# An expert's Silu moved one matmul step forward, ahead of ScalarE's weight splits of that step

## The chip, the core and the metric

One core of a Trainium2 chip runs the whole program. The metric is the device time of one execution in microseconds (us), lower is better. A step or a wait named below is one of this core's engines: TensorE (PE, with its weight loads as PEld), VectorE (DVE), ScalarE (ACT), GpSimd (POOL) and SyncE (SP, which issues the large DMAs).

## What is computed

A two-layer trunk over 256 frames of width 1024. The first layer is a mixer and a dense SwiGLU; the second is stick-breaking attention and a mixture of eight experts, of which each frame uses two. The change touches the experts alone:

```python
def swiglu(x, w1, w3, w2):
    return (jax.nn.silu(x @ w1) * (x @ w3)) @ w2

    # moe_swiglu, D_FF = 2816
    for e in range(N_EXPERTS):
        y = y + combine[:, e:e + 1] * swiglu(xf, w1[e], w3[e], w2[e])
```

## The kernel before

The experts are sorted by their number of frames into eight places q. At an even q ("big") the expert has room for 128 frames and works in two halves of its 2816 hidden columns; at an odd q ("small") it has room for 64 frames and works in one go. Each half, or each small expert, is a phase n: twelve phases, of which 2, 5, 8 and 11 are small. Each phase has an up part and a down part, and the list `WORK` interlaces them: up 0, up 1, down 0, up 2, down 1, up 3, down 2, and so on. So after up n comes down n-1, except at the start, where up 1 follows up 0 directly.

An up part has 16 steps j. Step j takes one block of 128 rows (j // 2) of one matrix (j % 2: 0 is the gate matrix w1, 1 is w3). The gate matrix gathers in PSUM banks 0 to 2, w3 in banks 3 to 5. Step 14 completes the gate matrix, step 15 completes w3. A down part has 11 steps for a big expert and 22 for a small one.

For big experts every weight block is split into a rounded part and a remainder, so that a float32 product is made of three faster ones (L571 to L573). ACT writes the rounded part (`split_step_hi`, L831), then DVE the remainder (`split_step_lo`, L1842). The room for split blocks is small. The planner `place_units` therefore says for each block after which step its room is free, and the table `BEHIND[s]` lists the blocks that ACT and DVE split after step s. Small experts use their weights unsplit (L1664, L1685).

ACT and DVE walk through the same list of steps as PE, each with its own program order. After up n they do three things. ACT applies Silu to the gate banks and writes `u_act` (`silu_up(n)`, L1076, three instructions at L1080 of 512, 512 and 384 columns). DVE multiplies `u_act` by the w3 banks (`gate_up(n)`, L2266, L2270). PE turns the result by transposes (`turn_up(n)`, L1621) ahead of step 3 of the down part of a big expert, or step 4 of a small one. In phase 0 there is no down part in between: PE's step 0 of up 1 waits for `silu_up(0)`, because it overwrites the gate banks, and its step 1 waits for `gate_up(0)`, because it overwrites the w3 banks.

Both calls stand at the first step after up n, and so behind the blocks of `BEHIND` of step 15. By the planner's table five phases have blocks listed behind steps 14 and 15 of their up part:

| phase n | behind step 14 | behind step 15 |
|---|---|---|
| 0 | up 1 step 2 | up 1 step 3 |
| 1 | down 0 step 2 | down 0 steps 3, 4 |
| 4 | down 3 step 3 | down 3 step 4 |
| 7 | down 6 steps 2, 3 | down 6 step 4 |
| 10 | down 9 steps 2, 3 | down 9 steps 4, 5 |

In the other seven phases nothing is listed behind step 15. SP issues the weight loads in order. Each waits until the ring space that it overwrites is free: `lo_done` counts remainders written by DVE, `raw_used` counts steps of small experts done by PE (L643).

Of the kernel before, what the change touches and what calls it, by code (L numbers as in the profile page):

```python
# [22 lines left out]
def trunk(nc, x, e_norm1, e_w_in, e_sgu_ln_g, e_sgu_ln_b, e_sgu_w, e_sgu_b, e_conv_w, e_a_log,  # L23
# [4 lines left out]
    TILES, DC = SEQ // P, D // P  # L28
# [75 lines left out]
    def big(q):  # L104
        return q % 2 == 0
# [9 lines left out]
    STEPS, PIECES, n_big, n_raw = [], [], 0, 0  # L115
# [96 lines left out]
    def place_units():  # L212

        taken = [((i % SPLITS) * DC * CW, (i % SPLITS + 1) * DC * CW, i) for i in range(A_MOE - SPLITS, A_MOE)]
        at, spot, behind = (A_MOE % SPLITS) * DC * CW, {}, {}
        raws_needed = [raws for _, _, raws in WHERE]
        raw_step = [s for s, st in enumerate(STEPS) if not st.big]
        step_of = {A_MOE + st.at: s for s, st in enumerate(STEPS) if st.big}
        for s, st in enumerate(STEPS):
            if not st.big:  # L220
                continue
            if at + st.size > SPLIT_ROOM:
                at = 0
            last = max(claim(taken, at, at + st.size, A_MOE + st.at))
            spot[st.at] = (at, last)
            raws = max(raws_needed[:st.pieces[0][0] + 1])
            free = step_of.get(last, last - A_MOE)
            if raws:
                free = max(free, raw_step[raws - 1])
            if s > st.j and not STEPS[s - st.j - 1].big:  # L230
                start = s - st.j
                free = max(free, start if st.kind == "down" and st.j >= 4 else start - EARLY if st.kind == "up" else 0)
            behind.setdefault(free, []).append(s)
            at += st.size
        return spot, behind
# [14 lines left out]
    with ExitStack() as ctx:  # L250
# [269 lines left out]
        def stepped(eng, st):  # L520

            if st.big:
                eng.wait_ge(piece_used, A_MOE + st.at + 1)
            else:
                eng.wait_ge(raw_used, st.at + 1)

        def last_step(kind, n):
            return next(st for st in STEPS if st.kind == kind and st.n == n and st.ends)
# [8 lines left out]
        def gather_bank(q, b):  # L537
            return 6 + b if q == 0 else 3 + b
# [13 lines left out]
        def finished_before(st):  # L552

            v = STEPS.index(st)
            if st.j == 0 and v and STEPS[v - 1].kind == "down":
                p = STEPS[v - 1]
                if LAST[p.q] == p.n:
                    return p.q
            return None
# [219 lines left out]
        def _(act):  # L779
# [46 lines left out]
            def split_step_hi(st):  # L826

                (v, off), = st.pieces
                act.wait_ge(ring_in[arrive_sem(v)], arrive_count(v))
                used(act, SPOT[st.at][1])  # L830
                act.activation(unit(all_hi, st), in_ring(WHERE[v][0] + off, st.size), ACT.Copy).then_inc(hi_done, 1)  # L831
# [230 lines left out]
            def gathered(q):  # L1062

                for b in range(2):
                    act.wait_ge(gather_done, 2 * q + b + 1)
                    src = ps[:, gather_bank(q, b), :]
                    if big(q):
                        ins = act.activation(xg_hi[:, 4 * b:4 * b + 4, :], src.rearrange("p (c n) -> p c n", c=4), ACT.Copy)
                    else:
                        ins = act.activation(xg_raw[:, 4 * b:4 * b + 4, :], src[:, 0:4 * SMALL].rearrange("p (c n) -> p c n", c=4),  # L1070
                                             ACT.Copy)
                    ins.then_inc(xgh_ready, 1)

            def silu_up(n):

                stepped(act, last_step("up", n))  # L1076
                if n:
                    act.wait_ge(hT_done, TURN0 + PARTS * n)
                for b, (c0, w) in enumerate(UP_COLS):
                    act.activation(u_act[:, c0:c0 + w], ps[:, b, 0:w], ACT.Silu).then_inc(silu_done, 1)  # L1080

            def turned_hi(n, parts=range(PARTS)):

                for b in parts:
                    act.wait_ge(hT_done, TURN0 + PARTS * n + b + 1)
                    blocks = turn_blocks(b)
                    src = ps[:, turn_bank(n, b), 0:P * len(blocks)].rearrange("p (j n) -> p j n", n=P)
                    m = m_hi if big(PHASE[n][0]) else m_raw
                    act.activation(m[n % 2][:, blocks[0]:blocks[-1] + 1, :], src, ACT.Copy).then_inc(hTh_ready, 1)

            def finished(q):

                stepped(act, last_step("down", LAST[q]))
                if big(q):
                    ins = act.activation(y_exp[:, 512:D], ps[:, 7, :], ACT.Copy)
                else:
                    ins = act.activation(y_small[SMALL:P, :], ps[SMALL:P, 6, :], ACT.Copy)
                ins.then_inc(y_act, 1)

            gathered(0)  # L1100
            for s, st in enumerate(STEPS):
                if finished_before(st) is not None:
                    finished(finished_before(st))
                if st.kind == "up" and st.n == 1:
                    if st.j == 0:
                        silu_up(0)
                    if st.j == 3:
                        turned_hi(0, (0, 1))
                    if st.j == 7:
                        turned_hi(0, (2,))  # L1110
                if st.kind == "down" and st.n + 1 < PHASES:
                    q = PHASE[st.n + 1][0]
                    if st.j == 0:
                        silu_up(st.n + 1)
                    if st.j == TURN_AT[st.big]:
                        turned_hi(st.n + 1)
                    if st.j == GATHER_AT and LAST[q] == st.n + 1 and q + 1 < NE:
                        gathered(q + 1)
                for k in BEHIND.get(s, ()):
                    split_step_hi(STEPS[k])  # L1120
            finished(NE - 1)
# [673 lines left out]
        def _(vec):  # L1795
# [469 lines left out]

            def gate_up(n):  # L2266

                for b, (c0, w) in enumerate(UP_COLS):
                    vec.wait_ge(silu_done, ACT0 + PARTS * n + b + 1)
                    tt(u_act[:, c0:c0 + w], u_act[:, c0:c0 + w], ps[:, 3 + b, 0:w], ALU.mult).then_inc(act_ready, 1)  # L2270
# [19 lines left out]
            def finished(q):  # L2290

                stepped(vec, last_step("down", LAST[q]))
                if big(q):
                    ins = vec.tensor_copy(y_exp[:, 0:512], ps[:, 6, :])
                else:
                    ins = vec.tensor_copy(y_small[0:SMALL, :], ps[0:SMALL, 6, :])
                ins.then_inc(y_vec, 1)
# [12 lines left out]
            for s, st in enumerate(STEPS):  # L2310
# [13 lines left out]
                if st.kind == "up" and st.n == 1:  # L2324
                    if st.j == 0:
                        gate_up(0)
                    if st.j == 3:
                        turned_lo(0, (0, 1))
                    if st.j == 7:
                        turned_lo(0, (2,))  # L2330
# [111 lines left out]
```

## Time and profile before

| | |
|---|---|
| median of 3 runs | 1226.92 us (1224.8 to 1231.65) |
| the profiled execution, its own time | 1229.17 us |
| its span, first to last instruction | 1227.1 us |
| PE busy | 1162.8 us, 95% of the span |
| DVE busy | 665.1 us, 54% |
| ACT busy | 559.7 us, 46% |
| mean granted TensorE clock | 0.986 |
| HBM read | 348.89 MB |

The experts take roughly the second half of the span, from 511 us on. In that half the page shows 360 to 416 GB/s in most of its slices of 30.7 us, so that PE and the DMA engines look full at the same time. A mean over a slice can't tell which of the two is waiting for the other. For that the rows below are read: they name single waits, single instructions and short stretches.

### The profile page before, as it was taken

What the parts mean: (1) busy time and instruction counts of PE and PEld (TensorE: products, weight loads), DVE (VectorE), ACT (ScalarE), POOL (GpSimd) and SP (SyncE); (2) the same over time, 40 slices, a digit from 0 to 9 for tenths busy, and PEclk for the clock granted to TensorE, in tenths of its full rate; (3) what the DMA queues carried; (4) which work ended last, traced back from release to release, by engine and by line L of the source; (5) the groups of instructions that cost most, each with busy time, mean ns of one, the idle gap of its engine ahead of it and who ended that gap; (6) DMA issues with size and microseconds to landing.
All of it is one profiled execution on the core that took longest, in us unless ns stands there. A gap on an engine that the chain in (4) does not pass through costs nothing.

```text
span 1227.1 us, 16270 instructions
## 1 busy us (share of the span) xinstructions
PE 1162.8 (95%) x6555; PEld 858.4 (70%) x6555; DVE 665.1 (54%) x736; ACT 559.7 (46%) x638; POOL 49.6 (4%) x93
## 2 busy tenths in 40 slices
PE   5989899999999999899998999999999989999986
PEld 5979778888879886778637748548568368386351
DVE  4866655545455422797507658038476058474053
ACT  4772454344444565476407547036355056263041
POOL 8010000000000121000000000000000000000000
PEclk9999999999999999899999999999999989999998
DMA  9632259655554421298799999999999999998993
GB/s 318 185 105 71 69 183 364 209 191 182 177 170 151 166 71 64 89 360 292 263 416 413 411 414 413 397 412 414 411 398 377 374 412 412 401 412 323 416 409 128
DMA packets 116736, 351.07 MB, mean 286 GB/s; under 512 B 8136, under 2 KB 55280, under 8 KB 116656
## 3 DMA queue, kind: packets, MB, share of 16 engines
q1 hardware_dynamic: 115552, 347.11, 74.3%
q0 software_dynamic: 1104, 2.86, 0.8%
q8 instruction: 54, 0.88, 0.3%
q14 instruction: 26, 0.21, 0.0%
HBM read 348.89 MB, written 1.05 MB: 285 GB/s over the span
## 4 chain that ended last, share of the span: by engine, by line
PE 84%; DMA 6%; DVE 4%; ACT 3%; POOL 2%; issue 1%; POOLq 0%; SPq 0%; DVEq 0%; ACTq 0%
PE ps L571 20%; PE ps L573 19%; PE ps L572 19%; PE ps L1664 8%; PE ps L1685 6%; DMA arena_c<-in_o_moe_w_dram 5%; PE ps L1609 3%; PE ps L1646 2%; DVE all_lo L1842 1%; PE ps L1621 1%; PE ps L1318 1%; POOL level L689 1%; PE ps L1526 1%; ACT all_hi L831 1%; PE ps L1538 1%
## 5 line engine op out<-in xcount | busy, mean ns | idle before, releaser
L1842 DVE TENSOR_TENSOR all_lo<-arena_c,all_hi 128x1408 fp32r<-128x1408 f32 (+1 forms) x120 | 170.7, 1448 | 217.4 <-ACT all_hi L831 217.3
L831 ACT ACTIVATE all_hi<-arena_c 128x1408 fp32r<-128x1408 f32 (+1 forms) x120 | 146.5, 1246 | 246.3 <-DMA arena_c<-in_o_moe_w_dram 199.9
L1842 DVE TENSOR_TENSOR all_lo<-arena_a,all_hi 128x1408 fp32r<-128x1408 f32 (+1 forms) x96 | 138.2, 1471 | 24.7 <-ACT all_hi L831 24.4
L571 PE MATMUL ps<-all_hi,xg_hi 128*128 128x512 f32 (+1 forms) x384 | 144.9, 377 | 2.9 <-ACT u_act L1080 2.9
L573 PE MATMUL ps<-all_hi,xg_lo 128*128 128x512 f32 (+1 forms) x384 | 144.8, 377 | 0.0
L831 ACT ACTIVATE all_hi<-arena_a 128x1408 fp32r<-128x1408 f32 (+1 forms) x96 | 119.2, 1262 | 56.0 <-PE ps L573 35.3
L572 PE MATMUL ps<-all_lo,xg_hi 128*128 128x512 f32 (+1 forms) x384 | 144.4, 376 | 0.0
L571 PE MATMUL ps<-all_hi,x_hi 128*128 128x512 f32 (+1 forms) x336 | 124.2, 370 | 5.1 <-ACT xn L920 2.4
L1835 DVE TENSOR_TENSOR all_lo<-arena_a,all_hi 128x2048 fp32r<-128x2048 f32 x40 | 91.4, 2289 | 58.0 <-ACT all_hi L824 58.0
L573 PE MATMUL ps<-all_hi,x_lo 128*128 128x512 f32 (+1 forms) x336 | 120.8, 360 | 0.0
L572 PE MATMUL ps<-all_lo,x_hi 128*128 128x512 f32 (+1 forms) x336 | 120.7, 359 | 0.0
L1664 PE MATMUL ps<-arena_c,xg_raw 128*64 128x512 f32 (+1 forms) x408 | 91.9, 558 | 0.3 <-DMA arena_c<-in_o_moe_w_dram 0.2
L571 PE MATMUL ps<-x_hi,all_hi 128*128 128x256 f32 x288 | 84.4, 293 | 4.3 <-DVE x_lo L1828 3.3
L824 ACT ACTIVATE all_hi<-arena_a 128x2048 fp32r<-128x2048 f32 x40 | 76.5, 1914 | 25.6 <-PE ps L573 21.7
L1664 PE MATMUL ps<-arena_a,xg_raw 128*64 128x512 f32 x360 | 82.9, 558 | 2.3 <-DMA arena_a<-in_o_moe_w_dram 2.3
L571 PEld LDWEIGHTS ps<-all_hi,xg_hi 128*128 128x128 f32 x384 | 72.5, 189 | 16.8 <-ACT u_act L1080 3.2
L571 PE MATMUL ps<-all_hi,m_hi 128*128 128x512 f32 x176 | 73.7, 419 | 9.9 <-DVE all_lo L1842 9.9
L572 PE MATMUL ps<-x_lo,all_hi 128*128 128x256 f32 x288 | 82.6, 287 | 0.0
L573 PE MATMUL ps<-x_hi,all_lo 128*128 128x256 f32 x288 | 82.6, 287 | 0.0
L572 PEld LDWEIGHTS ps<-all_lo,xg_hi 128*128 128x128 f32 x384 | 72.5, 189 | 11.9
L573 PEld LDWEIGHTS ps<-all_hi,xg_lo 128*128 128x128 f32 x384 | 72.5, 189 | 11.3
L1835 DVE TENSOR_TENSOR all_lo<-arena_c,all_hi 128x2048 fp32r<-128x2048 f32 x25 | 57.3, 2291 | 35.8 <-ACT all_hi L824 35.8
(367 smaller groups left out, 1782.2 us busy)
## 6 DMA issues: line engine op xcount, KB each, us to landing
arena_c<-in_o_moe_w_dram SPq DMA_DIRECT2D x136, 704.0 KB, 9.9
arena_a<-in_o_moe_w_dram SPq DMA_DIRECT2D x120, 704.0 KB, 9.8
arena_c<-in_o_moe_w_dram SPq DMA_DIRECT2D x45, 1024.0 KB, 15.3
arena_a<-in_o_moe_w_dram SPq DMA_DIRECT2D x35, 1024.0 KB, 16.1
arena_c<-in_e_ffn_w_dram SPq DMA_DIRECT2D x36, 512.0 KB, 6.9
arena_a<-in_e_ffn_w_dram SPq DMA_DIRECT2D x30, 512.0 KB, 5.1
arena_a<-in_e_w_in_dram SPq DMA_DIRECT2D x24, 512.0 KB, 8.8
arena_a<-in_o_w_qkv_dram SPq DMA_DIRECT2D x12, 512.0 KB, 4.5
```

The source lines that it names most:

```text
L571: pe.matmul(o, a_hi, b_hi, start=first, stop=False)
L572: pe.matmul(o, a_hi, b_lo, start=False, stop=False)
L573: return pe.matmul(o, a_lo, b_hi, start=False, stop=last)
L689: after(pool.affine_select(out=t, in_=t, pattern=pattern, compare_op=op, fill=fill, base=base, channel_multiplier=cm))
L824: act.activation(w_hi[i % SPLITS][:, :], ring[slot][:, :], ACT.Copy).then_inc(hi_done, 1)
L831: act.activation(unit(all_hi, st), in_ring(WHERE[v][0] + off, st.size), ACT.Copy).then_inc(hi_done, 1)
L1609: last = mm(ps[:, gather_bank(q, c // 4), at:at + n], xn[:, t, c * P:(c + 1) * P], sel_p[:, t, 0:n], start=(t == 0), stop=(t == TILES - 1))
L1646: mm(ps[:, SCAT[q][m], :], a, y, start=True, stop=True).then_inc(scat_done, 1)
L1664: last = mm(ps[a * SMALL:(a + 1) * SMALL, o + b, 0:n], xg_raw[:, c, :], raw[a][:, c0:c0 + n], start=(c == 0), stop=(c == DC - 1))
L1685: last = mm(ps[hf * SMALL:(hf + 1) * SMALL, 6, :], m_raw[st.n % 2][:, j, st.a * SMALL:(st.a + 1) * SMALL], raw[:, hf * 512:(hf + 1) * 512] ...
L1835: tt(w_lo[i % SPLITS][:, :], ring[slot][:, :], w_hi[i % SPLITS][:, :].bitcast(F32), ALU.subtract).then_inc(lo_done, 1)
L1842: tt(unit(all_lo, st), in_ring(WHERE[v][0] + off, st.size), unit(all_hi, st).bitcast(F32), ALU.subtract).then_inc(lo_done, 1)
```

## The change

`silu_up(n)` waits for step 14 of up n (found by the new `gates_step(n)`) instead of step 15. In ACT's program it moves from the first step after up n to step 15 of up n itself, ahead of the blocks that `BEHIND` lists there. `gate_up(n)` stays where it is in DVE's program. Since Silu no longer implies that w3's banks are complete, it gets a wait of its own for step 15.

```diff
+        def gates_step(n):
+            return next(st for st in STEPS if st.kind == "up" and st.n == n and st.part == (DC - 1, 0))
+
         def last_step(kind, n):
...
             def silu_up(n):
 
-                stepped(act, last_step("up", n))
+                stepped(act, gates_step(n))
                 if n:
                     act.wait_ge(hT_done, TURN0 + PARTS * n)
...
                 if st.kind == "up" and st.n == 1:
-                    if st.j == 0:
-                        silu_up(0)
                     if st.j == 3:
                         turned_hi(0, (0, 1))
...
                 if st.kind == "down" and st.n + 1 < PHASES:
                     q = PHASE[st.n + 1][0]
-                    if st.j == 0:
-                        silu_up(st.n + 1)
                     if st.j == TURN_AT[st.big]:
                         turned_hi(st.n + 1)
...
+                if st.kind == "up" and st.j == 2 * DC - 1:
+                    silu_up(st.n)
                 for k in BEHIND.get(s, ()):
                     split_step_hi(STEPS[k])
...
             def gate_up(n):
 
+                stepped(vec, last_step("up", n))
                 for b, (c0, w) in enumerate(UP_COLS):
```

## Rows read from the trace of the kernel before

**Rows 1.** PE's waits, 540 to 1215 us: waiting, awaited, total, times, longest.

```profile
PE ps L571 <- DVE all_lo L1842: 9.9, 4, 3.0
PE ps L1621 <- DVE u_act L2270: 3.6, 4, 1.4
```

**Rows 2.** Windows: PE, PEld, DVE, ACT, POOL busy; clock, DMA share, GB/s.

```profile
604.00:606.00 2.00, 2.00 (x10) 1.53 (x9) 0.00 (x0) 0.00 (x0) 0.00 (x0) 1.00 0.01 3
...
780.00:782.00 2.00, 2.00 (x12) 0.72 (x10) 0.00 (x0) 0.00 (x0) 0.00 (x0) 1.00 0.72 237
...
1126.00:1128.00 2.00, 2.00 (x10) 1.05 (x10) 0.00 (x0) 0.00 (x0) 0.00 (x0) 1.00 0.00 0
```

**Rows 3.** ACT's timeline: start, us, line, out<-in, count, idle before and releaser.

```profile
546.55 1.39 ACT L831 ACTIVATE all_hi<-arena_c 128x1408 fp32r<-128x1408 f32 x1 [0.53 <-PE ps L573]
548.46 1.38 ACT L831 ACTIVATE all_hi<-arena_c 128x1408 fp32r<-128x1408 f32 x1 [0.53 <-PE ps L573]
...
583.06 1.06 ACT L831 ACTIVATE all_hi<-arena_c 128x1024 fp32r<-128x1024 f32 x1 [0.85 <-PE ps L573]
...
586.89 1.45 ACT L1080 ACTIVATE u_act<-ps 128x512 f32<-128x512 f32 x3
588.21 1.07 ACT L831 ACTIVATE all_hi<-arena_c 128x1024 fp32r<-128x1024 f32 x1
...
752.89 2.98 ACT L831 ACTIVATE all_hi<-arena_a 128x1024 fp32r<-128x1024 f32 x3 [0.85 <-PE ps L573]
...
927.64 2.98 ACT L831 ACTIVATE all_hi<-arena_c 128x1024 fp32r<-128x1024 f32 x3 [0.85 <-PE ps L573]
...
1103.66 2.01 ACT L831 ACTIVATE all_hi<-arena_a 128x1024 fp32r<-128x1024 f32 x2 [0.85 <-PE ps L573]
```

**Rows 4.** DVE's timeline around the ends of up 0, 1, 4, 7, 10.

```profile
549.87 1.63 DVE L1842 TENSOR_TENSOR all_lo<-arena_c,all_hi 128x1408 fp32r<-128x1408 f32 x1 [0.29 <-ACT all_hi L831]
551.42 1.74 DVE L2270 TENSOR_TENSOR u_act<-u_act,ps 128x512 f32<-128x512 f32 x3
...
586.07 2.36 DVE L1842 TENSOR_TENSOR all_lo<-arena_c,all_hi 128x1024 fp32r<-128x1024 f32 x2 [0.69 <-ACT all_hi L831]
...
757.82 1.23 DVE L1842 TENSOR_TENSOR all_lo<-arena_c,all_hi 128x1024 fp32r<-128x1024 f32 x1 [0.34 <-ACT all_hi L831]
...
928.74 3.50 DVE L1842 TENSOR_TENSOR all_lo<-arena_c,all_hi 128x1024 fp32r<-128x1024 f32 x3 [0.69 <-ACT all_hi L831]
...
1107.03 2.35 DVE L1842 TENSOR_TENSOR all_lo<-arena_c,all_hi 128x1024 fp32r<-128x1024 f32 x2
```

**Rows 5.** PE's timeline where PE first uses what Silu and the gate give.

```profile
551.25 0.80 PE L571 MATMUL ps<-all_hi,xg_hi 128*128 128x512 f32 x1 [2.88 <-ACT u_act L1080]
...
554.79 0.40 PE L571 MATMUL ps<-all_hi,xg_hi 128*128 128x512 f32 x1
...
590.15 1.42 PE L1621 MATMUL ps<-ident,u_act 128*128 128x128 f32 x11 [1.08 <-DVE u_act L2270]
...
760.76 0.98 PE L1621 MATMUL ps<-ident,u_act 128*128 128x128 f32 x7
...
933.95 1.31 PE L1621 MATMUL ps<-ident,u_act 128*128 128x128 f32 x10 [0.30 <-DVE u_act L2270]
...
1111.10 1.42 PE L1621 MATMUL ps<-ident,u_act 128*128 128x128 f32 x11 [1.43 <-DVE u_act L2270]
```

**Rows 6.** Windows behind five of PE's gaps; the clock is the third number from the end.

```profile
551.00:554.60 3.60, 3.35 (x8) 2.80 (x9) 2.16 (x4) 0.19 (x1) 0.00 (x0) 0.53 0.97 319
...
648.50:652.00 3.50, 3.50 (x15) 2.87 (x16) 3.30 (x4) 3.43 (x6) 0.00 (x0) 1.00 1.03 410
...
817.60:821.00 3.40, 3.37 (x8) 2.70 (x9) 3.19 (x3) 3.27 (x6) 0.00 (x0) 0.52 1.03 411
...
1111.00:1114.50 3.50, 3.40 (x21) 3.00 (x22) 3.50 (x5) 2.77 (x5) 0.00 (x0) 1.00 1.02 415
...
1169.00:1172.40 3.40, 3.40 (x10) 2.62 (x9) 3.33 (x4) 3.40 (x7) 0.00 (x0) 0.50 1.02 404
```

## The prediction

> **What bounds the kernel now.** I read three kinds of view in this order: the waits of PE, then short windows of the DMA engines, then the timelines of ACT and DVE where up parts end. PE is the engine that matters in the expert stage, and its list of waits is short [rows 1]: four waits for a weight remainder, 9.9 us together, and four transposes that waited for the gate product, 3.6 us together. The reader should see what is missing there. Silu itself is named nowhere in the list but once, at the end of up 0, where PE stood idle for 2.88 us [rows 5].
>
> The DMA engines look full over the stage, but they run dry behind every big expert. At 604 us they moved 3 GB/s, at 780 us they fell to a share of 0.72, and at 1126 us they moved nothing [rows 2]; a stretch like the first stands near 950 us. In those stretches SP waits for ring space that a small expert's steps free, so PE sets when the stream starts again. What PE loses between two such stretches therefore moves the next stream, the arrival of the next weights, and the end. I count each such loss in full.
>
> **What the change moves.** No instruction is added or removed. The three Silu instructions keep their cost: they start at 586.89 and the next instruction at 588.21, so they occupy ACT for 1.32 us, and the last ends after 1.45 us [rows 3]. No DMA is issued by what is moved, and no other queue is passed. What changes is the order on ACT: Silu now stands ahead of the splits behind step 15. DVE's order stays: remainders of the blocks behind step 15 first, then the gate product. So the gate product no longer waits for a late Silu, but a remainder ahead of it waits for a rounded part that now stands behind Silu. In seven phases nothing is listed behind step 15. There ACT's order is as before and PE's transposes wait either for nothing or for remainders; I take 0 for them. DVE's added wait is for a step that Silu used to wait for; queued behind it are the gate product and later remainders, which have the same condition already. A further hop between engines is about 0.05 us, so the five waits are 0 to 0.25 us; I take 0, since each is met before the remainder ahead of it is done.
>
> **Phase 0.** Before, ACT splits at 546.55 and 548.46, one PE step of 1.91 us apart, and Silu follows the second [rows 3]. Now it follows the first, so PE starts up 1 at 551.25 - 1.91 = 549.34 and its gap shrinks from 2.88 to 0.97 us. That is the gain that one would expect. But step 1 of up 1 waits for the gate product. The second split now starts at 546.55 + 1.29 + 1.32 = 549.16 instead of 548.46, 0.70 us later (1.29 is a split's 1.38 less the 0.09 by which the next instruction overlaps it). Its remainder on DVE starts at 549.87 + 0.70 = 550.57 and the gate product at 551.42 + 0.70 = 552.12; it takes 1.74 us [rows 4], so PE may begin step 1 at 553.91. PE has finished step 0 at 549.34 + 1.91 = 551.25 and now waits 2.66 us there.
>
> Before, step 1 began at 554.79 [rows 5], because step 0 ran slowly: from 551 to 554.6 us, behind the gap of 2.88, a clock of 0.53 was granted, that is mostly the 1.2 GHz level [rows 6]. So step 0 took 554.79 - 551.25 = 3.54 us, 1.63 more than a full-speed step, and step 1 ended at 556.70. If the clock falls behind the new gap too, step 1 ends at 553.91 + 3.54 = 557.45, which is +0.75. If it does not, it ends at 555.82, which is -0.88. The new gap of 2.66 is nearest to the old one of 2.88, so I take +0.75 and keep -0.88 for the range.
>
> **Phases 1, 4, 7 and 10.** The same sum four times: when does the first split behind step 15 start, if Silu's 1.32 us are put ahead of it?
>
> Phase 1: the split behind step 14 starts at 583.06 and is followed by Silu 0.97 us later, at 584.03. The next split starts at 585.35, its remainder 1.10 us later (split and hand-over, 583.06's kind) at 586.45, against 586.07 [rows 3, 4]: +0.38. The transposes at 590.15 had waited 1.08 us for the gate product [rows 5], so PE is late by all of it.
>
> Phase 4: three splits from 752.89 end at 755.87; Silu begins at 755.78, the next split at 757.10, its remainder at 758.20 against 757.82: +0.38. PE reached these transposes at 760.76 without a wait; the gate product would end at about 761.08 and PE start 0.04 later, so +0.36.
>
> Phase 7: of the three splits from 927.64 two are behind step 14. They occupy ACT until 929.57, Silu until 930.89, and the third's remainder starts at 931.99. Before, it was the third of a run of three from 928.74 that took 3.50 us, so it began at 931.02 [rows 4]: +0.97. The transposes had waited 0.30 us already.
>
> Phase 10: two splits from 1103.66 occupy ACT until 1105.58, Silu until 1106.90, and the third remainder starts at 1108.00 against 1107.03: +0.97. The transposes' wait grows from 1.43 to 2.40 us.
>
> What hides none of this: in all four cases the gate product stands directly behind these remainders on DVE, and PE directly behind the gate product. If PE had slack there, it would show no idle time ahead of the transposes; only phase 4 shows none.
>
> The sum is 0.75 + 0.38 + 0.36 + 0.97 + 0.97 = 3.43 us.
>
> **The clock behind the fourth wait.** PE's gap of 2.40 us in phase 10 is one the trace of before does not have at that place. Behind 1.43 us there the clock stayed at 1.00. Of the four waits for a remainder the longest took 3.0 of 9.9 us [rows 1], so the other three took 2.3 each. The windows from 648.5, 817.6 and 1169 us lie behind those three: 1.00 was granted in the first, 0.52 and 0.50 in the others [rows 6]. So two of three fell. The price is between 0 and 1.63 us; by those rows, the nearest in length, I take two thirds, 1.1 us. Total 3.43 + 1.1 = 4.5 us.
>
> Against the profiled execution that is 1229.17 + 4.5 = 1233.7. That execution lies 2.25 us above the median of the runs, inside their scatter, so for the median I add the same sum: 1226.92 + 4.5 = **1231.4 us**.
>
> **The rivals.** First, the stream of weights absorbs it. For this speak the full DMA windows outside the dry stretches; against it the three windows where the engines stood or sagged. It would give no change, 1226.9 us. The Trainium skill, page "Perfetto Trace Analysis", section "Roofline", says that a single core can pull about 120% of its 358 GB/s share and is then held by its 16 DMA engines. By that rule a stage this full is set by its bytes, and PE's microsecond would cost nothing. The trace agrees on the rate, with 410 to 415 GB/s in three of the windows read for the clock [rows 6], but not on the conclusion, since the rate falls to 3 and 0 in others.
>
> Second, the first boundary keeps the full clock, or the splits behind it are less delayed than I think: phase 0 gives -0.88 instead of +0.75, and the sum falls to 1.8, or 2.9 with the clock's part: 1228.7 to 1229.8 us.
>
> Third, the expected gain arrives. PE starts up 1 earlier by 1.91 us at full clock, saving 1.63 more, and the later delays are absorbed: -3.5, or 1223.4 us. For it speaks the one wait for Silu, against it the order on DVE, which puts a remainder ahead of the gate product.
>
> Fourth, on the slow side: the clock. It decides in phases 1, 7 and 10, where PE's gaps grow to 1.46, 1.27 and 2.40 us. If it falls behind all three, that is 3 x 1.63 = 4.9 on top of 3.43, so +8.3 and 1235.3 us. From two falls on, the sum passes 6.1 us. Against it: behind 1.43 us at 1111 it did not fall.
>
> **How the numbers follow.** 0.5% is 6.1 us, about what a measurement of this kernel can tell from no change. Forecast 0.55, first rival 0.10, second 0.14, third 0.08, fourth 0.13. The runs of before scatter from 1224.8 to 1231.65, so the forecast's upper part, some 0.13, and most of the fourth lie over 1233.1: slower 0.24. Faster by over 6.1 us only the third could give, and only with scatter: 0.05. The rest, 0.71, is within. The range from 1226.0 to 1236.0 takes in the forecast with both ends of the clock's price, the first two rivals and the fourth.
>
> **What would show it.** In the trace after: Silu's three instructions at about 547.8 and PE's start of up 1 near 549.3; a second gap of about 2.7 us ahead of step 1 of up 1, named as a wait for the gate product; waits of transposes for the gate product of 1.5, 0.4, 1.3 and 2.4 us in phases 1, 4, 7 and 10; dry stretches of the DMA engines that each begin and end later by the sum so far. The prediction is wrong if the remainders behind step 15 start no later than before, if the second gap in phase 0 is missing, or if the dry stretches end where they did while PE's waits have grown.

## The result, and the profile after

| | before | after |
|---|---|---|
| median | 1229.38 us (1223.76 to 1232.55, 9 runs) | 1237.11 us (1234.13 to 1238.85, 9 runs) |
| ratio | | 1.0071, 95% interval 1.005 to 1.0091 |
| profiled execution, span | 1227.1 us | 1236.5 us |
| instructions in it | 16270 | 16282 |

The change makes the kernel slower by 8.7 us (6.1 to 11.2). The forecast was 4.5 us: the right sign, half the size, and the time lies above the stated range. The ratios here and below compare the executions as a whole; the microseconds beside them follow the ratio and differ from the difference of the two medians by up to 1.2 us. The three Silu instructions do what the diff says. What they cost, and what else the change brought along, is read in the profile after. Its span is 9.4 us longer.

PE's timeline after, at the places of [rows 5], with the first matmul of the expert stage ahead of them and the last scatter behind:

```profile
514.28 0.98 PE L1610 MATMUL ps<-sel_p,xn 128*128 128x128 f32 x3 [0.42 <-DVE sel_p L2179]
...
552.34 0.50 PE L574 MATMUL ps<-all_hi,xg_hi 128*128 128x512 f32 x1 [0.97 <-ACT u_act L1083]
...
556.93 0.54 PE L574 MATMUL ps<-all_hi,xg_hi 128*128 128x512 f32 x1 [2.42 <-DVE u_act L2272]
...
594.35 1.42 PE L1622 MATMUL ps<-ident,u_act 128*128 128x128 f32 x11 [1.46 <-DVE u_act L2272]
...
766.16 1.42 PE L1622 MATMUL ps<-ident,u_act 128*128 128x128 f32 x11 [0.46 <-DVE u_act L2272]
...
940.56 1.42 PE L1622 MATMUL ps<-ident,u_act 128*128 128x128 f32 x11 [1.41 <-DVE u_act L2272]
...
1117.22 2.61 PE L1622 MATMUL ps<-ident,u_act 128*128 128x128 f32 x11 [2.55 <-DVE u_act L2272]
...
1222.86 1.99 PE L1647 MATMUL ps<-y_small,back_last 64*128 64x512 f32 x8 [0.89 <-DVE y_small L2298]
```

The gap before up 1 has shrunk from 2.88 to 0.97 us, and a second one of 2.42 us has opened behind it, which waits for the gate product. Ahead of the transposes the gaps have grown from 1.08, 0, 0.30 and 1.43 to 1.46, 0.46, 1.41 and 2.55 us.

ACT after, at the end of up 0:

```profile
547.63 1.39 ACT L834 ACTIVATE all_hi<-arena_c 128x1408 fp32r<-128x1408 f32 x1 [0.53 <-PE ps L576]
549.55 1.39 ACT L834 ACTIVATE all_hi<-arena_c 128x1408 fp32r<-128x1408 f32 x1 [0.53 <-PE ps L576]
550.85 1.44 ACT L1083 ACTIVATE u_act<-ps 128x512 f32<-128x512 f32 x3
552.16 1.40 ACT L834 ACTIVATE all_hi<-arena_c 128x1408 fp32r<-128x1408 f32 x1
```

DVE after, the same stretch:

```profile
553.59 1.63 DVE L1843 TENSOR_TENSOR all_lo<-arena_c,all_hi 128x1408 fp32r<-128x1408 f32 x1 [0.99 <-ACT all_hi L834]
555.13 1.74 DVE L2272 TENSOR_TENSOR u_act<-u_act,ps 128x512 f32<-128x512 f32 x3
```

The reader should see the order: split, Silu, split on ACT; and on DVE an idle time of 0.99 us that waits for the second of these splits, with the gate product behind it. The w3 banks had been complete since PE's last matmul of up 0 (552.34 - 0.97 = 551.37), Silu was done at 552.29, and the product began at 555.13.

At the end of the program ACT waits for VectorE's queue, in the profile before and then after:

```profile
1219.37 1.06 ACT L794 ACTIVATE xn<-h 128x1024 f32<-128x1024 f32 x1 [2.05 <-DVEq L2411]
```

```profile
1228.81 1.06 ACT L797 ACTIVATE xn<-h 128x1024 f32<-128x1024 f32 x1 [4.31 <-DVEq L2413]
```

That is 2.26 us more. VectorE jumps here over the loop for further items, which is not entered. From the end of the jump's record to VectorE's next one pass 0.53 us before and 2.82 us after. Its last addition runs on for 0.6 us from there in both profiles: before, that covers the jump, and after, VectorE computes nothing for the other 2.2 us.

The third place lies ahead of the experts, where the change does nothing. The first matmul of the expert stage stands at 514.28 after and in the next row before:

```profile
511.09 1.20 PE L1609 MATMUL ps<-sel_p,xn 128*128 128x128 f32 x4 [0.42 <-DVE sel_p L2178]
```

Windows after (columns as in [rows 2]; the clock is the third number from the end) show two stretches at the 1.2 GHz level there, behind gaps of 2.37 and 2.27 us that both kernels have, and two more behind gaps that the change made:

```profile
89.60:92.80 3.20, 3.20 (x18) 2.98 (x18) 0.00 (x0) 0.00 (x0) 0.00 (x0) 0.50 0.02 5
147.60:150.80 3.20, 3.09 (x7) 2.48 (x8) 3.20 (x2) 0.00 (x0) 0.00 (x0) 0.51 0.65 194
557.20:560.40 3.20, 3.20 (x10) 2.67 (x10) 1.21 (x1) 0.00 (x0) 0.00 (x0) 0.51 0.93 328
...
1117.00:1120.20 3.20, 2.98 (x13) 2.88 (x14) 3.20 (x4) 1.53 (x3) 0.00 (x0) 0.51 1.02 417
```

Before, the clock stayed up at the first two:

```profile
88.50:91.50 3.00, 3.00 (x35) 2.87 (x35) 0.00 (x0) 0.84 (x1) 0.00 (x0) 1.00 0.02 5
146.50:149.50 3.00, 3.00 (x13) 2.26 (x13) 3.00 (x2) 0.00 (x0) 0.00 (x0) 1.00 0.80 260
```

So the span's 9.4 us divide into 3.19 ahead of the experts (514.28 - 511.09), 3.99 within them (1222.86 - 1215.68 - 3.19, the last scatter of before being at 1215.68), and 2.26 at the jump. Whether the first and the last belong to the change is for the runs to say.

### The profile page after: what moved, and what is told of

It reads as the page before. It is cut to its first block, busy times and chain, and to the rows that moved or that the text cites. A ratio compares the mean times of both kernels' runs of the same rounds, so it can differ in the third digit from the quotient of the medians.

```text
span 1236.5 us, 16282 instructions
## 1 busy us (share of the span) xinstructions
PE 1164.7 (94%) x6555; PEld 860.0 (70%) x6555; DVE 665.4 (54%) x736; ACT 560.2 (45%) x638; POOL 49.7 (4%) x93
## 4 chain that ended last, share of the span: by engine, by line
PE 83%; DMA 6%; DVE 4%; ACT 3%; issue 2%; POOL 2%; POOLq 0%; SPq 0%; ACTq 0%; DVEq 0%
PE ps L574 19%; PE ps L576 19%; PE ps L575 19%; PE ps L1665 8%; PE ps L1686 6%; DMA arena_c<-in_o_moe_w_dram 4%; PE ps L1610 3%; PE ps L1647 2%; PE ps L1622 1%; DMA arena_a<-in_o_moe_w_dram 1%; PE ps L1319 1%; ACT all_hi L834 1%; DVE u_act L2272 1%; POOL level L692 1%; PE ps L1527 1%
## 5 line engine op out<-in xcount | busy, mean ns | idle before, releaser
L574 PEld LDWEIGHTS ps<-all_hi,xg_hi 128*128 128x128 f32 x384 | 72.6, 189 | 17.1 <-DVE u_act L2272 2.7
L574 PEld LDWEIGHTS ps<-all_hi,x_hi 128*128 128x128 f32 x336 | 64.3, 191 | 17.9 <-issue 5.6
```

The lines of the kernel that those rows point to most:

```text
L574: pe.matmul(o, a_hi, b_hi, start=first, stop=False)
```

## The experiments

Theory A says that two things belong to the change. On ACT, a split that DVE's gate product indirectly waits for now stands behind Silu. And the twelve waits added on VectorE lengthen the jump at the end. Theory B puts the loss on the added waits in the experts; theory C calls the end chance; a fourth puts 3 us ahead of the experts. All runs carry out the whole computation.

**Only the waits.** The kernel before, and in it

```diff
             def gate_up(n):
 
+                stepped(vec, last_step("up", n))
                 for b, (c0, w) in enumerate(UP_COLS):
```

> The kernel before, with nothing of the change but the wait for step 15 ahead of each of the twelve gate products on VectorE; Silu stands where it stood. Theory A (the changed kernel loses in two places: about 4 us in the experts through the order on ScalarE, and 2.3 us at the end, where VectorE's jump over the unused loop takes 2.9 us instead of 0.6 because twelve more instructions moved its target): the experts keep the gaps of before (2.88 us before up 1, 1.08, 0.30 and 1.43 us before the transposes of phases 1, 7, 10), the jump takes about 2.9 us, and the time is 2.3 us above before. Theory B (the added waits cost in the experts): the transposes' gaps grow and the jump stays at 0.6 us. Theory C (the 2.3 us at the end are chance): nothing moves, time as before.

Measured: 1231.45 us against 1229.52, ratio 1.0019 (1.0008 to 1.003), which is +2.3 us. PE's gaps before up 1 and before the transposes of phases 1, 7 and 10 are 2.88, 1.08, 0.30 and 1.43 us, those of before. All waits of transposes for the gate product make 4.8 us against 3.6 [rows 1]; the rest lies in small phases, where gaps of about 0.8 us come and go in every kernel (6.2 us in all in "the target of the jump" below, which executes the instructions of before). The end is that of the changed kernel:

```profile
1222.75 1.06 ACT L794 ACTIVATE xn<-h 128x1024 f32<-128x1024 f32 x1 [4.30 <-DVEq L2412]
```

The waits cost nothing that can be seen where they stand, and 2.3 us at the jump. B and C fall.

**Only the order.** The changed kernel without the waits on VectorE:

```diff
-                stepped(act, gates_step(n))
+                stepped(act, gates_step(n) if SPLIT_AFTER(n) else last_step("up", n))
...
             def gate_up(n):
 
-                stepped(vec, last_step("up", n))
```

`SPLIT_AFTER(n)` is true for phases 0, 1, 4, 7 and 10. There a remainder ahead of the gate product on VectorE already implies step 15.

> The change's order on ScalarE without the added VectorE instructions. Silu stands ahead of the splits of step 15; in the five phases with splits there it waits for step 14, in the other seven for step 15 as before, so that the gate products need no wait of their own. Theory A: PE's gaps are those of the changed kernel (0.97 us before up 1 and 2.4 us before its step 1; 1.46, 0.46, 1.41 and 2.55 us before the transposes of phases 1, 4, 7, 10), the jump at the end takes 0.6 us, and the time lies 3 to 6 us above before and 2.3 us below the changed kernel. Theory B (the added waits carry the loss): gaps and time as before. A theory in which 3 us of the loss lie ahead of the experts whatever the instructions: 6 to 8 us above before.

Measured: 1234.37 us, ratio 1.0046 (1.0032 to 1.006), +5.6 us. PE's gaps are those of the changed kernel: 0.96 and 2.44 in phase 0, then 1.47, 0.47, 1.41 and 2.55. ACT's wait for the jump is 2.05 us as before. In this profile the first matmul of the experts stands at 511.20, with no stretch of low clock behind those two gaps: the 3.19 us of the other profile are not of the change. Over the twelve profiles of this document this place follows the number of such low stretches between 22 and 505 us and not the edit: 511.1 to 511.2 with none, 512.4 to 513.1 with one, 514.3 to 515.2 with two, 515.6 with three. Order and waits together make 1.0065; the change measured 1.0071.

**The complement: the gate product first.** In the changed kernel VectorE's order is changed in the same way:

```diff
-                    if st.j == 0:
-                        gate_up(0)
...
-                        if st.j == 0:
-                            gate_up(following)
...
+                if st.kind == "up" and st.j == 2 * DC - 1:
+                    gate_up(st.n)
                 for k in BEHIND.get(s, ()):
                     split_step_lo(STEPS[k])
```

> The changed kernel, with VectorE's order changed in the same way: the gate product of up n stands ahead of the remainders behind step 15, with its wait for step 15. Theory A (what costs is the remainder that stands ahead of the gate product and now waits for a rounded part behind Silu): the wait of 2.4 us before step 1 of up 1 falls under 0.5 us, the transposes' gaps in phases 1, 4, 7 and 10 go to about 0, the jump at the end keeps its 2.9 us; up 1 gains about 3.5 us and the transposes 2.8 us on the kernel before, the end gives 2.3 us back: about 4 us below before. Rival (PE then waits for the late remainders themselves): gaps of 1 us or more appear ahead of down steps 3 or 4 or of up 1 step 3, and the time is no lower than before.

Measured: 1225.05 us, ratio 0.9966 (0.9953 to 0.9979), -4.2 us. This is PE's list of waits, 540 to 1215 us:

```profile
PE ps L574 <- DVE all_lo L1843: 10.3, 4, 3.3
PE ps L1665 <- DMA arena_a<-in_o_moe_w_dram: 1.7, 2, 0.9
PE ps L1686 <- DVE y_exp L2296: 1.0, 1, 1.0
PE ps L574 <- ACT u_act L1083: 1.0, 1, 1.0
...
PE ps L1622 <- DVE u_act L2272: 0.8, 1, 0.8
```

The wait before step 1 of up 1 is gone, and of the transposes' waits one of 0.8 us is left; it lies in phase 5, where nothing is listed behind step 15. The list of the changed kernel had 2.4 and 7.6 us in these two rows. No wait for a late remainder has come in their place: 10.3 us against 9.9 in [rows 1]. The remainder ahead of the gate product is the cause of the order's loss. The end is as slow as the twelve waits make it: here the jump took 3.05 us.

**The target of the jump.** The kernel before, with twelve waits in the loop that is jumped over:

```diff
                     k = vec.value_load(item_i[0:1, 1, bass.ds(it, 1)], min_val=0, max_val=NK - 1)
+                    for _ in range(12):
+                        vec.wait_ge(items_ready, 1)
                     prep_item(it, k)
```

> The kernel before with twelve waits added inside VectorE's loop for further items, which is not entered here: nothing more is executed, only the target of the jump over the loop lies twelve instructions further on. If the place of the target decides how long the jump takes: about 2.9 us instead of 0.6, time 2.3 us above before. If the place of the jump itself decides, or the number of instructions executed: 0.6 us, time as before.

Measured: 1230.57 us, ratio 1.0001 (0.9987 to 1.0015); ACT's wait 2.05 us, the jump 0.53. A target that alone lies twelve instructions further on costs nothing here.

**The gate product first, Silu at its old time.** As the complement, but with

```diff
-                stepped(act, gates_step(n))
+                stepped(act, last_step("up", n))
...
             def gate_up(n):
 
-                stepped(vec, last_step("up", n))
```

> Silu ahead of the splits behind step 15 and the gate product ahead of the remainders behind step 15, but Silu waits for step 15 as in the kernel before, so no wait is added on VectorE. Theory A (the remainder ahead of the gate product costs the experts' part, twelve added waits the end): the gap before up 1 is about 1.6 us instead of 0.97, none before its step 1, none before the transposes of phases 1, 4, 7 and 10; the jump at the end takes 0.6 us. Time about 6 us below before, and 1.5 us below the kernel with the gate product first and the waits. If the earlier start of Silu were what pays: a time like before.

Measured: 1224.76 us, ratio 0.9954 (0.9937 to 0.997), -5.7 us. The gap before up 1 is 1.56 us, and the transposes of phases 1, 4, 7 and 10 wait for nothing. So with Silu ahead of the splits the order on VectorE carries the gain, and Silu's earlier wait is worth 0.6 us at most, at up 1. VectorE's order changed alone, with Silu behind the splits, was not tried.

**The gate product first, waits in five phases only.** As the complement, with

```diff
-                stepped(act, gates_step(n))
+                stepped(act, gates_step(n) if SPLIT_AFTER(n) else last_step("up", n))
...
-                stepped(vec, last_step("up", n))
+                if SPLIT_AFTER(n):
+                    stepped(vec, last_step("up", n))
```

> Both orders changed as in the kernel with the gate product first; Silu waits for step 14, and VectorE has its wait for step 15, only in the five phases with splits behind step 15. Five instructions are added on VectorE instead of twelve. Gaps as in that kernel: 0.97 us before up 1 and none before the transposes. If the jump's cost comes in a step as its place moves on, it is 0.5 or 2.8 us and nothing between; if it grows with each instruction, about 1.5 us. Time 6.5 us below before in the first case, 4.3 in the second, 5.3 in the third.

Measured: 1222.89 us, ratio 0.9956 (0.994 to 0.9972), -5.4 us. This and the run ahead of it beat both kernels and can't be told apart. Five added instructions leave the jump at 0.53 us, so its cost does not grow with their number:

```profile
1213.13 1.06 ACT L800 ACTIVATE xn<-h 128x1024 f32<-128x1024 f32 x1 [2.05 <-DVEq L2415]
```

At the end of up 10, where the change had made the longest of the transposes' gaps, DVE now does two remainders, the gate product, then the rest:

```profile
1099.81 2.36 DVE L1846 TENSOR_TENSOR all_lo<-arena_a,all_hi 128x1024 fp32r<-128x1024 f32 x2 [0.69 <-ACT all_hi L837]
1102.08 1.74 DVE L2276 TENSOR_TENSOR u_act<-u_act,ps 128x512 f32<-128x512 f32 x3
1103.74 5.76 DVE L1846 TENSOR_TENSOR all_lo<-arena_c,all_hi 128x1024 fp32r<-128x1024 f32 x5
```

**Phase 0 alone.** The order of "only the order", in phase 0:

```diff
+                if st.kind == "up" and st.j == 2 * DC - 1 and st.n == 0:
+                    silu_up(st.n)
```

> The change's order and its earlier wait in phase 0 alone; Silu of the other eleven phases as before, no wait added. Forecast of the prediction for this part: +0.75 us with the clock falling behind the second gap, -0.88 without, so between 0.9 us below and 0.8 us above before; the gaps before up 1 and before its step 1 are 0.97 and 2.4 us, the transposes' gaps those of before (1.08, 0.30 and 1.43 us in phases 1, 7, 10). If phase 0 carries the loss: 3 us or more above before.

Measured: 1229.98 us, ratio 1.0011 (0.9999 to 1.0024), +1.4 us. The gaps are 0.97 and 2.42 in phase 0 and those of before elsewhere. The interval holds the forecast of +0.75 and leaves out -0.88. In this profile the clock did not fall behind the gap of 2.42 us; this execution, at 1227.79 us, was the second fastest of twelve.

**The later phases alone.** The same with `st.n > 0`.

> The change's order in phases 1 to 11, phase 0 as before, no wait added. Forecast of the prediction for this part: 0.38 + 0.36 + 0.97 + 0.97 = 2.7 us, and up to 1.6 us more for the clock in phase 10: 2.7 to 4.3 us above before. Gaps before the transposes 1.46, 0.46, 1.41 and 2.55 us in phases 1, 4, 7 and 10; 2.88 us before up 1. If phase 0 carries the loss: time as before.

Measured: 1233.59 us, ratio 1.0035 (1.0022 to 1.0048), +4.3 us. The gaps are 2.88 before up 1, and 1.47, 0.47, 1.41 and 2.55 before the transposes. The two halves, 1.0011 and 1.0035, make the 1.0046 of the whole order.

**How far the slow jump reaches.** The kernel before with more waits ahead of each gate product, in two sizes, each executed once:

```diff
             def gate_up(n):
 
+                for _ in range(3):                     # and 7 in the second
+                    stepped(vec, last_step("up", n))
```

> The kernel before with three waits instead of one ahead of each of the twelve gate products on VectorE: 36 instructions added, all of them met at once. So far the jump at the end took 0.5 us with 0 and 5 added instructions and 2.8 us with 12. If it is a step at one place in the program that recurs only much further on, 2.8 us here would say that the slow stretch is at least 24 instructions long, 0.5 us that it is shorter. If it grew with the number of instructions: 8 us.

> The same with seven waits ahead of each gate product: 84 instructions added. If the jump's cost depends on where it lies in some block of the program, either 0.5 or 2.8 us; if it grows with the number of instructions: over 15 us. PE's gaps in the experts stay those of the kernel before.

The 36 and 84 waits became 24 and 48 executed instructions: three waits take two instructions, seven take four. With 24 the jump took 2.78 us, the time was 1233.01 against 1225.47 of before beside it; the jump explains 2.2 of these 7.5 us, and single executions scatter by as much as the rest. With 48 it took 0.53 us and 1223.98. In order of added instructions, 0, 5, 12, 24 and 48, the jump took 0.53, 0.53, 2.82 (3.05 with the gate product first), 2.78 and 0.53 us. It is quick or slow with nothing between, and does not grow with the number: what the instructions change is the place of the jump and of its target together.

## Why the prediction was right and wrong

**Wrong: what the change adds.** The step that failed says that no instruction is added and that VectorE's waits are worth 0. The diff itself adds a wait, and twelve of them are twelve instructions on VectorE: 16282 against 16270. I priced them where they stand, and there the price of 0 held. I did not ask what else they move. They move everything behind them in VectorE's program, and the jump at the end went from 0.53 to 2.82 us. Run alone, they cost 2.3 us of the 8.7. The trace of before held the jump, ahead of the [2.05 <-DVEq] above, but not a slow one, so its price could not have been read there. That a place in VectorE's program has a price could have been asked: the Trainium skill, page "Runtime: NRT & Kernel Launch", section "Instruction fetch mechanics", says that a taken branch whose target lies outside the window already loaded must fetch it first. By that rule the wait is a fetch. The traces fit that. They list the DMA packets that carry instructions ("q14 instruction" on the page of the profile), and in all twelve profiles one of 8192 bytes starts 0.96 to 1.42 us behind the end of the jump's record. In the eight with a quick jump VectorE has gone on before it starts. In the four with a slow one VectorE goes on 1.82 to 1.84 us after its start, and where it started 0.23 us later than in the profile after, with the gate product first, the jump took 0.23 us longer. Which engine's instructions such a packet holds the trace does not say, and why 12 and 24 added instructions make the jump wait, and 5 and 48 do not, stays open; a target moved alone by twelve did not bring it.

**Wrong too: the base.** I added the sum to 1226.92 us, the median of three executions. The nine executions of before in the result have a median of 1229.38, 2.46 us more. The measured 1237.11 lies 1.1 us above the range's end of 1236.0, so either of the two, the jump or the base, was enough to carry it out. The base was a matter of scatter and says nothing of the mechanism; the jump is the part of it that was missed.

**Right: the order, its places and nearly its size.** The forecast without the jump was 4.5 us; order alone measured 5.6 (3.9 to 7.4). The parts:

| step of the prediction | forecast | in the profile after, or in a run alone |
|---|---|---|
| gap before up 1 | 0.97 us | 0.97 |
| gap before its step 1 | 2.66 | 2.42 |
| gaps in phases 1, 4, 7, 10 | 1.46, 0.36, 1.27, 2.40 | 1.46, 0.46, 1.41, 2.55 |
| phase 0 | +0.75 | +1.4 (-0.1 to 3.0), run alone |
| phases 1, 4, 7, 10 with the clock's part | +3.8 | +4.3 (2.7 to 5.9), run alone |

The gap of 2.66 came out as 2.42 because step 0 took 0.26 us longer behind its own gap (552.34 to 554.51, where the second gap begins) than a step of 1.91; step 1 starts 4.59 us behind step 0, against 4.57 worked out. The gaps of phases 4, 7 and 10 were short by 0.10 to 0.15. I let Silu begin 0.09 us before the split ahead of it ends, as a split behind Silu does, but it began behind that end (ACT, end of up 10, after):

```profile
1108.66 2.01 ACT L834 ACTIVATE all_hi<-arena_a 128x1024 fp32r<-128x1024 f32 x2 [0.86 <-PE ps L576]
1110.70 1.47 ACT L1083 ACTIVATE u_act<-ps 128x512 f32<-128x512 f32 x3
1112.04 2.97 ACT L834 ACTIVATE all_hi<-arena_c 128x1024 fp32r<-128x1024 f32 x3
```

**The clock.** Behind phase 0's second gap it fell, as taken: 0.51 from 557.2 us after, and also in the profile of order alone, but not in that of phase 0 alone. From step 1 of up 1 to the transposes of phase 1 PE took 37.42 us after (594.35 - 556.93) and 35.36 before [rows 5], 2.06 more; the working gave 1.63 for the clock and 0.38 for phase 1. Behind phase 10's gap of 2.55 us it fell in the profile after and stayed up in those of order alone and of the later phases alone. These windows of order alone lie behind its phase 0 and its phase 10:

```profile
554.10:557.30 3.20, 3.20 (x10) 2.72 (x9) 1.03 (x1) 0.00 (x0) 0.00 (x0) 0.50 0.89 342
1115.20:1118.40 3.20, 3.20 (x20) 2.84 (x21) 3.20 (x3) 1.79 (x4) 0.00 (x0) 1.00 1.01 415
```

So the term of two thirds of a fall, 1.1 us, is not settled: with one fall in three profiles it would be about 0.5 us, and three profiles are few. That it fell in the profile after was luck for the forecast. The fourth rival, a fall behind gaps of 1.27 and 1.46 us, did not come. What a single profile adds is scatter: before had its own falls in the experts, which after did not have at the same places (behind 991.5 us before, for one). From 540 to 1215 us before spent 17.1 us at the lower level and after 13.6, so by an estimate before lost up to 1.7 us more to the clock (half of the difference). That is about what parts the 3.99 us of the experts in this pair from the 5.6 of order alone.

**The stream of weights absorbs none of it that can be seen.** The first rival was wrong as the dry stretches said. After, the DMA engines run dry at these places (columns as in [rows 2]):

```profile
608.00:610.00 2.00, 2.00 (x10) 1.59 (x9) 0.00 (x0) 0.00 (x0) 0.00 (x0) 1.00 0.01 3
784.00:786.00 2.00, 2.00 (x14) 0.74 (x12) 0.00 (x0) 0.00 (x0) 0.00 (x0) 1.00 0.32 84
956.00:958.00 2.00, 2.00 (x10) 0.74 (x10) 0.00 (x0) 0.00 (x0) 0.00 (x0) 1.00 0.00 0
...
1132.00:1134.00 2.00, 2.00 (x10) 1.63 (x9) 0.00 (x0) 0.00 (x0) 0.00 (x0) 1.00 0.01 6
```

They are the stretches of [rows 2] and the one near 950 us, 4 to 6 us later, as PE's transposes of phases 1, 4, 7 and 10 stand 4.2 to 6.6 us later; 3.2 of that came from ahead of the experts. The third rival, the expected gain, is real but needs DVE's order too: with the gate product first the kernel is 4.2 to 5.7 us faster than before.

## What to carry to other kernels

Before an instruction is moved ahead on one engine, follow what it pushes back to the next engine's queue, and ask what is queued behind that. Here Silu came earlier and its consumer later, because a remainder stood ahead of the consumer and waited for a split that Silu had pushed back; moving the consumer in the same way turned a loss of 5.6 us into a gain of 5.4 (order only, and the gate product first with waits in five phases). And a wait that is met at once is still an instruction: where a program has a jump, count how many are added ahead of it, and read the jump in the profile after.

## What the runs showed of the hardware

VectorE's taken jump over an unused loop took 0.53 us with 0, 5 or 48 instructions added ahead of it, 2.82 to 3.05 us with 12 and 2.78 with 24. Its target moved alone by 12 took 0.53. In each slow case VectorE went on 1.82 to 1.84 us after the start of a DMA packet of 8192 bytes that carries instructions; in each quick case it went on before that packet started.

TensorE's clock fell to the 1.2 GHz level behind gaps of 2.3 to 2.9 us in some executions and not in others, at the same place and with the same gap. Ahead of the down part behind up 2 (gaps of 2.32 and 2.33 us, at 648 us before and 653 after) it stayed up before and fell after; ahead of that behind up 11 (2.32 us, at 1168 and 1176 us) it fell before and stayed up after. Behind 2.55 us in phase 10 it fell in the profile after and not in that of order alone. Each fall cost about 1.6 us here, so by an estimate two executions of the same program can differ by several microseconds without any change; the nine of before span 8.8 us.
